# The down-projection's first operands: new homes, six pieces, and the last quad's convolution behind the second tile

## The reference, cut to what matters

```python
def conv_ffn(x, buf, w_up, conv_w, conv_b, w_down):
    u = x @ w_up                                        # 1024 -> 2 * 2816
    ext = jnp.concatenate([buf.astype(u.dtype), u], axis=1)
    c = conv_b
    for k in range(CONV_W):                             # causal, width 3
        c = c + ext[:, k:k + t] * conv_w[k]
    gate, val = jnp.split(c, 2, axis=-1)
    h = jax.nn.gelu(gate, approximate=True) * val
    return h @ w_down, ext[:, -(CONV_W - 1):]           # 2816 -> 1024

f, conv_p = conv_ffn(rmsnorm(xp, g_ffn_pre[l]), zero_buf, w_up[l], conv_w[l], conv_b[l], w_down[l])
xp = xp + rmsnorm(f, g_ffn_post[l])
```

## Time and profile before

| | us |
|---|---|
| median of 3 runs | 2682.62 |
| lowest and highest run | 2680.57 and 2683.72 |
| the profiled execution, its own time | 2682.53 |
| its span, first to last instruction | 2680.6 |
| mean granted TensorE clock, share of full speed | 0.976 |
| TensorE busy | 2558.2 (95%) |
| VectorE busy | 1971.0 (74%) |
| ScalarE busy | 1291.9 (48%) |
| GpSimd busy | 469.4 (18%) |

### The profile page before, as it was taken

The page is one execution under the profiler, slowest core; times in us unless marked ns, Lnnn a source line. Parts: engine busy times, 40 slices in busy tenths (PEclk is TensorE's granted clock), DMA queues, the critical chain, the costliest instruction groups (busy, mean ns, idle before and its releaser), DMA issues. The chain is left out here.

```text
span 2680.6 us, 42699 instructions
## 1 busy us (share of the span) xinstructions
PE 2558.2 (95%) x15719; PEld 2359.3 (88%) x15719; DVE 1971.0 (74%) x2597; ACT 1291.9 (48%) x2479; POOL 469.4 (18%) x367
## 2 busy tenths in 40 slices
PE   8999978899999989989999999899999989999997
PEld 7999945677777778979999999899999989999997
DVE  6877678787878846899888888888888734465454
ACT  5444358576766754435444443544444434244242
POOL 1111041243433334530000000000000011121111
PEclk9999989899999999989999999899999999999999
DMA  7666656444445443662332224122222353645633
GB/s 220 224 221 217 215 172 178 89 86 79 76 84 89 75 127 109 203 240 79 112 107 88 99 92 169 64 73 80 79 82 76 134 192 134 239 164 183 234 129 121
DMA packets 222210, 364.31 MB, mean 136 GB/s; under 512 B 56500, under 2 KB 159636, under 8 KB 220692
## 3 DMA queue, kind: packets, MB, share of 16 engines
q1 hardware_dynamic: 222004, 361.64, 44.2%
HBM read 264.12 MB, written 98.23 MB: 135 GB/s over the span
## 5 line engine op out<-in xcount | busy, mean ns | idle before, releaser
L2427 PE MATMUL mf_ps<-mf_rounded,mix_rest_rounded 128*128 128x264 f32 x4752 | 680.6, 287 | 13.4 <-DVE mf_rounded L2839 13.4
L2427 PEld LDWEIGHTS mf_ps<-mf_rounded,mix_rest_rounded 128*128 128x128 f32 x4752 | 625.8, 191 | 14.5 <-issue 13.2
L2450 PE MATMUL mf_ps<-mf_rounded,mix_rest_rounded 128*128 128x424 f32 (+1 forms) x2640 | 513.1, 356 | 11.1 <-DVE mf_rounded L2959 10.1
L2450 PEld LDWEIGHTS mf_ps<-mf_rounded,mix_rest_rounded 128*128 128x128 f32 x2640 | 496.5, 188 | 26.8 <-DVE mf_rounded L2959 9.8
L2954 DVE TENSOR_TENSOR mix_rest_rounded<-mf_area,mix_rest_rounded 128x1408 fp32r<-128x1408 f32 x80 | 129.9, 1624 | 256.4 <-ACT mix_rest_rounded L2677 256.4
L2427 PE MATMUL mf_ps<-mf_rounded,mf_rounded 128*128 128x264 f32 x1584 | 283.8, 288 | 10.2 <-DVE room_rounded L2839 7.0
L2330 POOL TENSOR_TENSOR mf_area<-mf_area 128x424 f32<-128x424 f32 (+1 forms) x104 | 172.4, 1658 | 585.2 <-ACT mf_area L2482 446.3
L2677 ACT ACTIVATE mix_rest_rounded<-mf_area 128x1408 fp32r<-128x1408 f32 x80 | 110.4, 1380 | 317.9 <-PE mf_ps L2450 292.5
L1643 PE MATMUL at_ps<-ahead_q,ahead_k 96*128 96x512 f32 (+8 forms) x1008 | 259.0, 366 | 0.9 <-DMA ahead_q<-la_turned_top 0.9
L1700 ACT ACTIVATE la_prob<-at_ps 128x512 f32<-128x512 f32 (+1 forms) x336 | 175.5, 522 | 156.9 <-PE at_ps L1643 143.1
L2427 PEld LDWEIGHTS mf_ps<-mf_rounded,mf_rounded 128*128 128x128 f32 x1584 | 232.2, 191 | 10.8 <-issue 10.8
(11 more groups left out here) (241 smaller groups left out, 4620.5 us busy)
## 6 DMA issues: line engine op xcount, KB each, us to landing
mf_area<-in_w_down SPq DMA_DIRECT2D x80, 704.0 KB, 4.1
mix_rest<-in_w_up SPq DMA_DIRECT2D x176, 256.0 KB, 2.7
pi_w_raw<-in_w_in SPq DMA_DIRECT2D x49, 512.0 KB, 6.2
mf_area<-h_scr SPq DMA_DIRECT2D x8, 1484.0 KB, 8.8
h_scr<-mf_area SPq DMA_DIRECT2D x22, 528.0 KB, 4.1
h_scr<-mf_area SPq DMA_DIRECT2D x22, 496.0 KB, 3.3
la_rec_all<-inv_scr SPq DMA_DIRECT2D x32, 256.0 KB
ahead_k<-kn_scr SPq DMA_DIRECT2D x28, 280.0 KB, 5.0
```

Source lines behind the costliest of these rows:

```text
L2427: mm = pe.matmul(pair[slots[i]][:, e], w[:, k], x[:, e * HB:(e + 1) * HB], start=(k == 0 and m == 0 and i < 6), stop=(k == KH - 1 and m == 2),
L2450: mm = pe.matmul(acc[:, t % 2, 0:n], w[:, half, k], x[kk][:, 0:n], start=(kk == 0 and e == 0), stop=(kk == KF - 1 and e == 2))
```

## The change

- **Homes.** `H_AT` is a new list in the order in which places come free, with `H_FREE`, which says for each k which product of quad 43 must be done before the rounding of block 0 may write there: product 1 for k = 0, product 2 for k = 1 to 4, 3 for 5 to 9, 4 for 10 to 12, 5 for 13 to 16, 6 for 17 to 21. Before, it was product 5 for k under 11 and product 6 behind. k = 0 has a home in `room` for block 0 (`h_first`) and another for later blocks (`h_later`, where the convolution works with `u`). No home of block 0 is one of the convolution's any more.
- **Pieces.** h is loaded in six groups of 5, 5, 2, 1, 2 and 7 tiles (before 6, 7, 2 and 7). The two places of `wd_raw` lie apart.
- **SP.** The first weights are issued at the start of quad 43, group 0 behind product 0, group 1 behind product 1, groups 2 to 4 and the second weights behind product 2, group 5 behind product 4. `x1d` of block 0 is loaded in tile 0 of block 1 instead of before block 0. The store of quad 43's h and the stores of the convolution's state go into tile 4 of block 0.
- **ACT and DVE.** The convolution of quad 43 leaves the preparation of block 0 and goes into its tiles: `tap`, `corner_out`, `tap` into tile 1, `conv` twice and `gelu` into tile 2, `glu` into tile 3. DVE's subtraction for the first weights moves ahead of `mix_right`, and three `h_low` instead of four stand ahead of `mix_upper_right`.
- **Squares.** The two places for the squares of the down-projection move (`sq_down`): `room` for block 0, the convolution's old `cv` for later blocks.

```diff
+        H_LATER = (35608, 35608 + TB)
+        H_AT = [lo + TB * x for lo, a, z in ((25432, 0, 5), (31792, 0, 4), (0, 0, 4), (6336, 0, 14), (0, 4, 14), (31792, 4, 9))
+                for x in range(a, z)]
+        H_FREE = (1,) + (2,) * 4 + (3,) * 5 + (4,) * 3 + (5,) * 4 + (6,) * 5
...
-        H_GROUPS = ((0, 6, 12288), (6, 13, 22464), (13, 15, 18048), (15, 22, 28824))
+        H_GROUPS = ((0, 5, 12272), (5, 10, 22456), (10, 12, 24576), (12, 13, 14392), (13, 15, 18048), (15, 22, 28824))
...
+        h_first = [rounded(room, TB * x, TB) for x in range(2)]
+        h_later = [rounded(area, at, TB) for at in H_LATER]
+        h_place = [rounded(area, at, TB) for at in H_AT]
...
             for q in range(QUADS):
                 nxt, turn, last = q + 2 < QUADS, q == KF - 1, q == QUADS - 1
+                if last:
+                    sp.wait_ge(h_out, stores_of_h(KF))
+                    load_down(0)
...
+                if last:
+                    load_h(0, 0)
+                if turn or last:
+                    sp.wait_ge(chunk_done, product(q, 1))
                 if turn:
-                    sp.wait_ge(chunk_done, product(q, 1))
                     load_right(1, T2, 2, 1)
+                if last:
+                    load_h(0, 1)
                 sp.wait_ge(chunk_done, product(q, 2))
...
                 if last:
-                    sp.wait_ge(h_out, stores_of_h(KF))
-                    load_down(0)
-                    load_h(0, 0)
-                    load_h(0, 1)
-                    load_h(0, 2)
+                    for g in range(2, 5):
+                        load_h(0, g)
                     load_down(1)
...
                 if last:
                     sp.wait_ge(chunk_done, product(q, 4))
-                    load_h(0, 3)
+                    load_h(0, 5)
...
-            load_x1(0)
             for b in range(BLOCKS):
...
-                    if b == 0 and m == 0:
+                    if b == 0 and m == 4:
                         keep_h(QUADS - 1)
...
+                    if b == 1 and m == 0:
+                        sp.wait_ge(sq_added, squares["down", 0, KD - 1] + 1)
+                        load_x1(0)
                         sp.wait_ge(h_out, stores_of_h(QUADS))
-                    if b < LAST and m in (2, 3, 4, 5):
+                    if b < LAST and m in (2, 3, 4):
                         if m == 2:
                             sp.wait_ge(h_split, KF * (b + 1))
-                        load_h(b + 1, m - 2)
+                        for g in range(2 * m - 4, 2 * m - 2):
+                            load_h(b + 1, g)
...
                 if b == 0:
-                    if k == 0:
-                        act.wait_ge(chunk_done, product(QUADS - 1, 5))
-                    if k == HALF:
-                        act.wait_ge(chunk_done, product(QUADS - 1, 6))
+                    if k == 0 or H_FREE[k] > H_FREE[k - 1]:
+                        act.wait_ge(chunk_done, product(QUADS - 1, H_FREE[k]))
...
+                        if b == 0 and m == 1:
+                            if half:
+                                corner_out(QUADS - 1)
+                                tap(QUADS - 1, 0)
+                            else:
+                                tap(QUADS - 1, 1)
+                        if b == 0 and m == 2 and half:
+                            gelu(QUADS - 1)
...
+                        if b == 0 and m == 2:
+                            conv(QUADS - 1, 0 if half else 1)
+                        if b == 0 and m == 3 and half:
+                            glu(QUADS - 1)
```

More of the change, by code:

```diff
@@ L2049, in mix_and_ffn, with square_place @@
                 squares["down", b, j] = len(squares)
+        def square_place(what):
+            return (sq_down[min(what[1], 1)] if what[0] == "down" else sq)[:, squares[what] % 2]
         NORMS = 2 * BLOCKS
@@ L2467, in _ @@
             pe.wait_ge(sq_made, last + 1)
-            pe.matmul(st[:, 0:n], ones[:], sq[:, last % 2, 0:n], start=False, stop=True).then_inc(summed, 1)
+            pe.matmul(st[:, 0:n], ones[:], square_place(("down", LAST, KD - 1))[:, 0:n], start=False, stop=True).then_inc(summed, 1)
         @block.scalar
@@ L2481, in square @@
                     act.wait_ge(sq_added, i - 1)
-                return act.activation(sq[:, i % 2, 0:tile.shape[-1]], tile, ACT.Square)
+                if what == ("down", 1, 0):
+                    act.wait_ge(h_made, QUADS)
+                return act.activation(square_place(what)[:, 0:tile.shape[-1]], tile, ACT.Square)
             def out_tile(b, j):
@@ L3001, in _ @@
                 if last:
-                    down_weights(0)
-                    for k in range(4):
+                    for k in range(3):
                         h_low(0, k)
```

63 lines of the change are left out of this document (26 added, 37 removed).

## The result

The changed kernel takes 2664.11 us (median of 6 runs, 2663.22 to 2666.18), the kernel before 2682.10 us (median of 6 runs, 2680.57 to 2683.81). The ratio is 0.9931, with a 95% interval of 0.9921 to 0.9941: between 15.8 and 21.2 us less. The forecast was 2668.4, with a range of 2666.8 to 2672.4. The direction and the place were right, the gain came out 4.3 us larger than forecast and larger than the range allowed.

The account below looks back on a forecast made before the run. PE alone was taken to bound the down-projection except at its start, output tile 0. Its two chunks at 6.55 + 6.37 = 12.92 us instead of 27.09 save 14.17: 2682.53 - 14.17 = 2668.4 us, range 2666.8 to 2672.4.

Parts of the forecast that it names:

- What bounds the kernel, and where: Down-projection bound by PE alone except at its start, where output tile 0's two chunks take 27.09 us with gaps and slow running.
- The loads: Ahead of block 0: h's last piece lands near 2139.6 us instead of 2146.2, the second weights near 2133.
- VectorE is late next, with 1.8 us of cover: Tile 0: DVE's subtractions end with chunk 2's weights at 2147.8 us, PE needs them at 2149.6.
- The convolution in tiles 1 and 2, x1 in block 1, the next blocks' loads: cost 0: Behind tile 0: the moved convolution, x1 load and six-piece loads stay hidden under PE and cost 0.
- The sum for tile 0: Tile 0's two chunks without a wait take 6.55 and 6.37, 12.92 us instead of 27.09; saved 14.17 us.
- Nothing else changes: Everything outside tile 0 keeps its time, so the execution would be 2682.53 - 14.17 = 2668.4 us.
- The scatter: Whole kernel: about 1.5 us between runs (2680.57 to 2683.72), giving the forecast's own range of 2666.9 to 2669.9.
- Rival A: Each of two added h pieces delays the last by 3.3 us, to 2146.2; loss 2.6, time 2671.0; chance 0.11.
- Rival B: Chunk 2's weights take 14.8 us to land; PE waits 5.1 us, loss 5.1 to 7.7, 2673.5 to 2676.1; chance 0.05.
- Rival C: ACT still begins rounding at 2134.0; DVE ends near 2148.8, before 2149.6; forecast's time, chance within its 0.80.
- Rival D: Weights queue behind next blocks' pieces, up to eight stalls in four blocks; at 17 us landing 2699.6; chance 0.02.

Follow-up runs that it names:

- Round_late: Changed kernel, but block 0's rounding waits for products 5 and 6 of the last quad again, homes as changed; 2664.83 us, ratio 0.9931.
- conv_back: Changed kernel, but the last quad's convolution stands again between k = 17 and k = 18 of block 0's preparation; 2670.43 us, ratio 0.9954.
- loads_late: Changed kernel, but the first weights and groups 0 and 1 of h are issued behind product 2 again; 2667.38 us, ratio 0.9947.
- pieces22: Changed kernel, with h loaded tile by tile, 22 transfers for a block instead of six, rounding still by whole groups; 2666.03 us, ratio 0.9942.
- x1_again: Changed kernel, plus one more load of x1's first block ahead of chunk 2's weights, the real load staying where moved; 2664.78 us, ratio 0.9938.
- all_back: Changed kernel with convolution place, late loads and late rounding undone together; new homes, six pieces and moved x1 stay; 2677.44 us, ratio 0.9984.
- before_again: The kernel before, unchanged, run once more; 2680.67 us, ratio 0.9994.
- before_sems: The kernel before with two more semaphores allocated and nothing else; 2680.74 us, ratio 0.9994.
- before_shift: The kernel before with the homes of k = 0 to 13 moved up by 32 bytes; 2680.61 us, ratio 0.9996.
- after_swap: Changed kernel with high and low parts of h swapped within each pair of homes; 2665.39 us, ratio 0.9942.
- before_swap: The kernel before with high and low parts of h swapped within each pair of homes; 2682.64 us, ratio 1.0002.

## Why the prediction was right or wrong, point by point

- **What bounds the kernel, and where.** Right. The whole of what the change aimed at lay between 2136.67 and 2163.76, and TensorE now runs through it.
- **The loads.** Right in the end. The last piece was forecast at 2139.6 in the clock of before; it was there by 2136.3 + 3.58 = 2139.9. The sum over the queues was added up wrongly (2127.3 + 11.1 is 2138.4, not 2139.5), but the other way, the piece's own time alone, gave 2139.1, and it landed 8.8 us after its issue where 7.8 was put in. The second weights were forecast at 2133 and were there by 2133.2.
- **VectorE is late next, with 1.8 us of cover.** Right: 1.9. Its end was forecast at 2147.8 and came at 2143.86 + 3.58 = 2147.4, but TensorE also came to chunk 2 0.2 us sooner. Round_late shows the same cover from its end: 2.2 us of delay cost 0.3 us.
- **The convolution in tiles 1 and 2, x1 in block 1, the next blocks' loads: cost 0.** Right; TensorE's only waits after tile 0 are the four for the norm, 1.2 us in all, as in the earlier trace rows.
- **The sum for tile 0.** 14.17 forecast, 14.38 measured. I had given the first chunk the 6.55 us of the earlier trace rows, which hold the run-out of its last matmul. It takes the pace of all the others. This term was 0.2 us too small.
- **"Nothing else changes."** This step failed: it puts the 39 tiles behind tile 0 at nothing. The homes of the operands are an edit to all 40 tiles, and I priced them by when they come free, never by what TensorE does with them. The tiles became 0.02 to 0.05 us shorter, and what lies behind tile 0 1.4 us in all. Swapping and shifting h's homes alone moved the pace by 0.04 and 0.02 us, so homes can do this. And conv_back, round_late, loads_late, pieces22, x1_again and all_back, which undo or alter the other parts of the change, all keep 12.70 and 12.46 us. That leaves the addresses. It is not shown that h's homes make the whole difference, since the places of the raw weights and of the squares moved too, and which property of an address counts is open beyond the 32-byte shift.
- **The scatter.** This is the other step that failed, and the larger part of the miss. The range's lower end was the forecast less 1.6 us, read off three runs. With the right terms for tile 0 and the tiles behind it, the forecast would have been 2682.53 - 15.8 = 2666.7, and the measured 2664.11 is still 2.6 below. Of this, 0.4 is the base: the median of six runs of the kernel before is 2682.10, not 2682.53. The other 2.2, by the rests, lie ahead of tile 0, where nothing was forecast to change. The same kernel before ran from 2677.5 to 2686.6 us in later sets, with medians of 2681.5 to 2683.0, and its copies without effect on their rest (before_again and before_sems, 22 runs) have 2680.67 and 2680.74; the changed kernel has 2664.11 and 2663.26. So the two are 16.6 to 19.8 us apart by the set that is taken, of which the rest explains 15.8. A range of 1.6 us was too narrow for that. How much of the remainder belongs to the change is open; nothing speaks for the semaphores as its cause.
- **Rival A** (pieces pay their fixed time in a row): refuted by pieces22. **Rival B** (late weights of chunk 2): in the changed kernel these weights had landed before ScalarE came to them. With x1 put back in front of them (x1_again) they took 9.1 us, not 14.8, and cost 0.2 us, not 5. **Rival C** (ACT begins as late as before): I gave it the forecast's time, and round_late puts it at 0.3 to 0.4 us more. My conclusion from it holds. **Rival D** (weights behind the next block's pieces): no wait of that kind in any block.

The shares of the 14.4 us: the convolution's place 6.6 alone, the early loads 3.1 alone, the early rounding 0.3 alone, 2.6 that come only when all three are undone, and 1.8 for the rest, nearly all of it the last tile's wait for the store of h.

## What to carry to other kernels

When the bound engine stands still at a change of stage, write down for each engine between the last thing that can't move (here the last mix) and the first that must be there (chunk 2's weights) the list of work in its order: this gave the end within 0.4 us and the cover within 0.1, and one entry in a wrong place of that order, the convolution, was worth 6.6 us. A change of addresses is an edit to every instruction that reads them: allow for it over the whole loop. And take the scatter of a forecast from sets of runs, not from three runs of one set. A gain is best read from a mark in the trace ahead of which nothing was changed: that was good to 0.2 us here, where medians of the same program differed by 2.

## What the runs showed of the hardware that I had not expected

- The place of a matmul's moving operand in SBUF changes its pace. With the same instructions and shapes, a tile of 66 matmuls took 12.70 (after), 12.71 (before_shift), 12.73 (before), 12.74 (after_swap) and 12.77 us (before_swap) in five arrangements of the operands: 192.4 to 193.5 ns a matmul, in blocks 1 to 3. Moving 28 of 44 operands by 32 bytes made a tile 0.02 us shorter, swapping neighbours 0.04 longer.
- TensorE's clock fell behind a gap of 4.78 us (12 matmuls in 4.13 us, clock 0.56) and behind one of 8.16 (12 in 4.61, and 3 more in 1.22), and not behind gaps of 1.48 to 1.57 (clock 1.00). So removing a gap of the longer kind gave back 1.8 to 2.8 us more than its length.
- Twenty-two transfers of 212 KB in place of six, seven of them for the last group, moved the last landing by 1.1 us.
